# A transformer block pair on one core: silus and table loads in the planner's account, grouped silus, sums and masks on VectorE, another order of projections

## The chip, the core and the metric

The kernel runs on one core of a Trainium2 chip. The core has TensorE (PE, matrix products), VectorE (DVE), ScalarE (ACT), GpSimd (POOL) and SyncE (SP, which issues DMAs here). Each has a queue of its own and works through it in order; semaphores tie the queues together. The metric is the time of one launch on the device in microseconds (us), the median of several runs.

## The reference, cut to what matters

Two blocks over a sequence of 512 tokens, model width 1024, all in float32.

```python
def first_block(x, ...):
    h = h + 0.5 * rmsnorm(swiglu(rmsnorm(h)))          # FFN 1, width 2816
    u = rmsnorm(h)
    z, xbc, dt_raw, q, k, v, gates = split(u @ w_in)   # "mix 1"
    xbc = silu(causal_dwconv(xbc, 4 taps) + b)         # x (2048), B, C (4 groups of 128)
    y = ssd_chunked(x, softplus(dt_raw), A, B, C) + D * x      # 32 heads in 4 groups, chunks of 128
    y = rmsnorm over each group of (y * silu(z))
    y_ssd = y @ w_branch
    y_att = rmsnorm(softmax(q1 k1) v - lam * softmax(q2 k2) v) @ w_att   # 8 heads, ALiBi, causal
    merged = sigmoid(g0) * y_ssd + sigmoid(g1) * y_att
    h = h + rmsnorm(merged @ w_out)
    h = h + 0.5 * rmsnorm(swiglu(rmsnorm(h)))          # FFN 2
def second_block(x, ...):                              # "mix 2", then FFN 3
    q, k, v = silu(causal_dwconv(...)); q, k = l2norm(q), l2norm(k)
    o_gdn = rmsnorm(gated_delta_rule_chunked(q, k, v, g, beta)) * silu(z)   # 8 heads, chunks of 64
    o_dsa = sparse attention over the top 128 keys of an indexer
    h = h + (sigmoid(ga) * o_gdn + sigmoid(gb) * o_dsa) @ w_out
    h = h + (silu(conv(gate)) * conv(val)) @ w_down    # FFN 3
    return rmsnorm(h)
```

In the chunked delta rule a unit triangular matrix of 64 x 64 is inverted by levels: each level multiplies masked parts of a matrix with the inverse found so far.

## The kernel before

Activations lie transposed, features on the 128 partitions and the 512 tokens along the free dimension. Each float32 product is made of three float32r products (high times high, high times low, low times high; L1651 to L1653), so a **panel**, 1024 x 128 of a weight, is 8 x 3 = 24 matmuls of 128 x 128 x 512. A panel comes by DMA into one of 3 buffers `raw`, ScalarE rounds it (L1992) and VectorE subtracts to get the low part (L2289, tile `hl`, 3 buffers).

The work of a core is a list of steps, `plan`. Each engine's program walks that list once and issues its part of each step, so the plan's order is the order of every queue. What is emitted when is decided while the kernel is built. In the FFNs it is a plain loop. In mix 1 and mix 2 `schedule` (L705) runs a **main stream**, the projections, and **side streams**, the chains of small operations behind them (`ssd_side`, `att_side`; `scan_side`, `prep_side`, `index_side`). It asks the side streams first; a side stream goes on when `ready` (L383) says that the step's inputs are there by the account and that neither VectorE's nor ScalarE's account is more than `AHEAD` ahead of TensorE's. Else two k-blocks (6 matmuls) of the main stream are emitted. The account is `clock`, one time for each engine, which `spend` (L371) moves on by the costs that `costs` and `COSTS` give for a step's kind; a kind that has no entry costs nothing, and what it makes counts as ready at once.

The main stream's order is a string (L24, L25): in mix 1 `t` projects dt, `g0` to `g3` the x, B and C of a group (4 + 1 + 1 panels, each followed by a convolution of 4 taps and a silu), `z0` to `z3` the gates of a group (4 panels), `a` and `c` an attention head (3 panels; `c` waits for the head four before it), `b` the branch product of a gated group (16 half panels; it waits until the group is gated), `E` and `F` output gates, and `r8` waits until 8 pages are free. In mix 2 `p` is a pair of delta-rule heads (6 panels), `z` the two gates of a pair (4), `x` and `k` the indexer and the keys and values, `d` a sparse head's query, `h` waits until a pair is prepared. Pages are tiles of 128 x 512 in SBUF: 35 in mix 1, 38 in mix 2. The panels of dt, z0 and B of group 0 are made in the passage before mix 1 and lie in pages (`ahead`).

A group's chain in mix 1: four transposes with a scaling by dt (`ssd_x`, VectorE L2475), C times B (`ssd_cb`, TensorE L1723), states, then four rounds over pairs of heads (`ssd_from`, `ssd_front`, `ssd_mask`, `ssd_y`, TensorE L1759), then `gate_group` (L931): y times silu(z), squares on ScalarE, three additions on GpSimd (`sum4`, L2910), a product with a matrix of ones on TensorE (`rstd`, L1690), logarithm and exponential on ScalarE, and the gated tiles. Attention of a head: scores (L1786), softmax on VectorE and ScalarE, transposes of the probabilities (`pv_turn`, TensorE L1772, copied out by ScalarE, L2167), product with v (`pv_mul`, L1778). In mix 2 `gdn_seed` and `gdn_level` mask a tile for each level on GpSimd (L2924, L2931).

ScalarE must have a table set loaded that holds the function it evaluates; `activate` (L1970) issues a load (L1973) where the set in place doesn't hold it. Silu, exponential with logarithm, and exponential with tanh lie in different sets.

Before, a convolution's silu is issued in the middle of the next panel, and z's silu reads the bank that the product is in:

```python
            if q == STEP:
                flush()
...
            G["z"].append(evict("silu_ev", b))
```

Of the kernel before, what the change touches and what calls it, by code (L numbers as in the profile page):

```python
# [7 lines left out]
F = mybir.dt.float32  # L8
# [24 lines left out]
TABLES = {ACT.Ln: ("natural_log_exp_and_others",), ACT.Exp: ("natural_log_exp_and_others", "exp_and_others"),  # L33
          ACT.Silu: ("silu_and_others",), ACT.Tanh: ("silu_and_others", "exp_and_others"), ACT.Sigmoid: ("silu_and_others",)}
# [88 lines left out]
def costs(s):  # L123
# [8 lines left out]
    if k == "rstd":  # L132
        return [("PE", 0.9 * len(s["src"]), "pe_norm.sum"), ("ACT", 0.7, "act_norm.ln"), ("ACT", 0.63, "act_norm.r")]
    if k == "squares":
        return [("ACT", 0.62, "act_norm.sq", n) for n in range(len(s["src"]))]
    if k == "att_front":
        return [("PE", 0.33 * w), ("DVE", 0.45 + 0.58 * w), ("ACT", 0.5 + 0.22 * w, "act_att.P", 1)]
# [13 lines left out]
    if k == "sp_front":  # L151
        return [("PE", 0.14 * w), ("DVE", 0.45 + 0.27 * w), ("ACT", 0.4 + 0.11 * w, "act_spa.P")]
# [8 lines left out]
    "silu_ev": [("ACT", 0.63, "act_ev.out")], "tanh_ev": [("ACT", 0.63, "act_ev.out")],  # L161
# [3 lines left out]
    "sum4": [("POOL", 1.4, "pool_norm.sum4", 0), ("POOL", 1.4, "pool_norm.sum4", 1), ("POOL", 1.4, "pool_norm.sum4", 2)],  # L165
# [7 lines left out]
    "decay": [("DVE", 0.7), ("ACT", 0.63), ("DVE", 0.42), ("ACT", 0.63), ("DVE", 0.7), ("ACT", 0.63), ("DVE", 2.7), ("ACT", 0.2),  # L173
              ("DVE", 1.7, "dve_ssd.scan"), ("ACT", 0.62), ("DVE", 0.69, "dve_ssd.aclo")],
    "decay_turn": [("PE", 1.6, "pe_ssd.decay"), ("DVE", 0.9, "dve_ssd.alast"), ("ACT", 0.25), ("DVE", 0.3),
                   ("ACT", 0.3, "act_ssd.ddec")],
# [4 lines left out]
    "ssd_front": [("PE", 0.59), ("DVE", 0.69, "dve_ssd.seg"), ("DVE", 0.43), ("ACT", 0.65, "act_ssd.E")],  # L181
# [3 lines left out]
    "ssd_from": [("PE", 1.6, "pe_ssd.off"), ("ACT", 0.65, "act_ssd.EA"), ("DVE", 0.56, "dve_ssd.EA"), ("DVE", 0.56, "dve_ssd.off")],  # L185
    "ssd_y": [("PE", 1.03, "pe_ssd.y"), ("DVE", 0.69, "dve_ssd.y")],
    "turn_v": [("PE", 0.45, "pe_att.turn_v"), ("ACT", 0.6, "act_att.V")],
    "narrow": [("DVE", 0.9), ("ACT", 0.63), ("DVE", 1.1), ("ACT", 0.63), ("DVE", 0.42), ("ACT", 0.63), ("DVE", 0.7), ("ACT", 0.63),
               ("DVE", 5.0, "dve_gdn.nar")],
    "narrow_turn": [("PE", 4.1, "pe_gdn.iw"), ("ACT", 2.2, "act_gdn.cols", 1), ("ACT", 0.6, "act_gdn.iw")],  # L190
    "l2": [("DVE", 0.75, "dve_gdn.l2")],
    "gdn_decay": [("PE", 1.0), ("DVE", 0.69, "dve_gdn.seg"), ("DVE", 0.43), ("ACT", 0.65, "act_gdn.gm")],
# [3 lines left out]
    "gdn_seed": [("DVE", 1.4, "dve_gdn.U0"), ("POOL", 1.35, "pool_gdn.A", 0), ("POOL", 1.35, "pool_gdn.A", 1)],  # L196
    "gdn_seed_turn": [("PE", 1.15), ("ACT", 0.6, "act_gdn.T")],
    "gdn_level": [("PE", 1.07, "pe_gdn.Y"), ("ACT", 0.6, "act_gdn.Y"), ("POOL", 1.3, "pool_gdn.mask")],
# [6 lines left out]
    "gdn_norm": [("ACT", 1.25), ("DVE", 1.0, "dve_gdn.sum"), ("ACT", 0.45), ("DVE", 1.4, "dve_gdn.on")],  # L205
# [15 lines left out]
def build(nc, d, out):  # L221
# [137 lines left out]
    clock = dict.fromkeys(("PE", "ACT", "DVE", "POOL"), 0.0)  # L359
    at = {}  # L360
# [10 lines left out]
    def spend(s):  # L371
# [4 lines left out]
        if s.kind == "split" and s.j - NHL in ends:  # L376
            t = max(t, when(("pe_gemm.mm", *ends[s.j - NHL])))
        for engine, us, *name in costs(s):
            t = clock[engine] = max(clock[engine], t + 0.06) + us
            if name:  # L380
                at[(name[0], s.id, name[1] if len(name) > 1 else 0)] = t
# [18 lines left out]
    waiting = []  # L400
# [36 lines left out]
    def ugemm(src):  # L437
# [39 lines left out]
    def group_rstd(src, which):  # L477
# [5 lines left out]
        qs[1].release(("pool_norm.sum4", s2, 0))  # L483
        qs[3].release(("pool_norm.sum4", s2, 1))
        qs[2].release(("pool_norm.sum4", s2, 2))
        yield from ready(("pool_norm.sum4", s2, 2), banks=1)
        r = rstd([(qs[0][:, :], [("pool_norm.sum4", s2, 2)])], which)
# [157 lines left out]
    def conv(b, wname, taps, col, ncol, bias, silu, to=None, half=0):  # L645
        p = fp.take()
        flush()
# [3 lines left out]
    def conv_taps():  # L651
        if waiting and "s" not in waiting[0]:
            w = waiting[0]
# [7 lines left out]
    def flush():  # L661
        conv_taps()
        if waiting:
            w = waiting.pop()
            step("conv_silu", c=w["s"])
            t = ("act_conv.silu", w["s"])
            if w["to"] is None:
                w["p"].t = [t]
            else:
                w["p"].release(t)  # L670
                w["to"].t = w["to"].t + [t]
# [100 lines left out]
    s_con = step("ids")  # L772
    S1 = {}
# [27 lines left out]
    def project_group(g):  # L801
# [12 lines left out]
        yield  # L814
        flush()
        G["C"] = C
        G["xs"] = xs
# [105 lines left out]
    def project_z(g):  # L923
        G = grp[g]
        G["z"] = []
# [305 lines left out]
    def project_zg(h):  # L1231
        b = yield from ugemm(W2[24 + h])
# [1842 lines left out]
```

## Time and profile before

| | |
|---|---|
| median of 3 runs | 2760.79 us (2757.55 to 2762.05) |
| the profiled execution | 2757.5 us, span 2755.7 us |
| mean granted clock of TensorE | 0.973 |
| busy: TensorE, VectorE, ScalarE, GpSimd | 94%, 56%, 40%, 2% |
| FFN 1, mix 1, FFN 2, mix 2, FFN 3 (us, about) | 12 to 385, 385 to 1212, 1212 to 1670, 1670 to 2345, 2345 to 2755 |
| table loads of ScalarE | 95 |

A row of the windows gives the busy time of each engine in a stretch; the length less TensorE's busy time is its idle time. The granted clock is the share of full speed, 2.4 GHz, at which TensorE was clocked in the stretch. In a timeline the number in brackets is the idle time of the engine before the row's first instruction, with the instruction that ended it.

### The profile page before, as it was taken

How to read it: one execution, taken by the hardware profiler on the slowest of the kernel's cores; microseconds unless marked ns; L12 is line 12 of the kernel's file. 1: busy time of each engine (PE TensorE's matmuls, PEld its weight loads, DVE VectorE, ACT ScalarE, POOL GpSimd, SP SyncE). 2: the span in 40 equal slices, each digit the busy share in tenths (PEclk: the TensorE clock that was granted, in tenths of full speed). 3: DMA queues.
4: the chain of work that ended last, by engine and by line, in shares of the span. 5: the costliest groups of instructions: out<-in, count | busy, mean ns of one | idle time of the engine just before them, and what ended most of it. 6: DMA issues, size and time to landing. Idle time of an engine off the chain costs nothing.

```text
span 2755.7 us, 33784 instructions
## 1 busy us (share of the span) xinstructions
PE 2583.9 (94%) x13762; PEld 2037.0 (74%) x13762; DVE 1534.9 (56%) x2406; ACT 1111.1 (40%) x1684; POOL 44.9 (2%) x44
## 2 busy tenths in 40 slices
PE   7999998988899899899999999899999997999998
PEld 6888876666677677587888887677677675888886
DVE  5444257555666455535544327688765454677732
ACT  4223234545344445634322225543433355444421
POOL 0000000000000000000000000000000000000000
PEclk9999999999999999999999999999999999999999
DMA  4233322111121222122222332111111111323332
GB/s 138 97 100 96 98 91 71 54 46 61 54 65 58 69 70 66 56 85 92 92 96 95 96 97 85 62 47 62 46 56 39 55 54 39 99 93 100 96 94 78
DMA packets 59193, 209.93 MB, mean 76 GB/s; under 512 B 6560, under 2 KB 6560, under 8 KB 59040
## 3 DMA queue, kind: packets, MB, share of 16 engines
q1 hardware_dynamic: 57600, 204.38, 23.3%
q10 hardware_dynamic: 1440, 3.41, 0.4%
q8 instruction: 109, 1.79, 0.3%
q14 instruction: 44, 0.36, 0.0%
HBM read 205.66 MB, written 2.10 MB: 75 GB/s over the span
## 4 chain that ended last, share of the span: by engine, by line
PE 71%; DVE 15%; ACT 10%; issue 3%; POOL 1%; DMA 0%; DVEq 0%; SPq 0%; ACTq 0%
PE bank L1651 20%; PE bank L1653 19%; PE bank L1652 19%; DVE hl L2289 3%; ACT L1973 3%; ACT hl L1992 2%; ACT fB L1975 2%; DVE fB L2417 2%; ACT fA L1975 2%; PE bank L1853 1%; PE bank L1690 1%; PE bank L1778 1%; DVE fA L2417 1%; PE bank L1666 1%; PE bank L1668 1%
## 5 line engine op out<-in xcount | busy, mean ns | idle before, releaser
L1651 PE MATMUL bank<-uR,hl 128*128 128x512 f32 x2160 | 883.4, 409 | 25.9 <-DVE uR L2301 11.8
L1652 PE MATMUL bank<-uR,hl 128*128 128x512 f32 x2160 | 850.0, 394 | 0.0
L1653 PE MATMUL bank<-uR,hl 128*128 128x512 f32 x2160 | 850.0, 394 | 0.0
L2289 DVE TENSOR_TENSOR hl<-raw,hl 128x1024 fp32r<-128x1024 f32 (+1 forms) x391 | 472.1, 1208 | 621.4 <-ACT hl L1992 620.3
L1651 PEld LDWEIGHTS bank<-uR,hl 128*128 128x128 f32 x2160 | 411.2, 190 | 145.7 <-issue 41.7
L1992 ACT CAST hl<-raw 128x1024 fp32r<-128x1024 f32 (+1 forms) x391 | 401.5, 1029 | 207.7 <-PE bank L1653 195.5
L1653 PEld LDWEIGHTS bank<-uR,hl 128*128 128x128 f32 x2160 | 410.4, 190 | 88.7
L1652 PEld LDWEIGHTS bank<-uR,hl 128*128 128x128 f32 x2160 | 411.5, 191 | 86.7 <-issue 6.6
L1651 PE MATMUL bank<-act,hl 128*128 128x512 f32 x528 | 206.6, 391 | 0.0
L1653 PE MATMUL bank<-act,hl 128*128 128x512 f32 x528 | 205.5, 389 | 0.0
L1652 PE MATMUL bank<-act,hl 128*128 128x512 f32 x528 | 205.4, 389 | 0.0
L1973 ACT ACT_TABLE_LOAD x95 | 121.9, 1283 | 182.7 <-DVE fB L2417 39.2
L2294 DVE TENSOR_TENSOR fA<-bank,fA 128x512 f32<-128x512 f32 x132 | 90.9, 690 | 137.4 <-PE bank L1653 133.7
L1975 ACT ACTIVATE fA<-fA 128x512 f32<-128x512 f32 (+1 forms) x120 | 75.5, 631 | 213.9 <-DVE fA L2294 123.7
L2059 ACT CAST act<-fA 128x512 fp32r<-128x512 f32 x66 | 41.0, 621 | 284.1 <-DVE fA L2384 194.0
L1651 PE MATMUL bank<-mR,hl 128*128 128x512 f32 x320 | 129.2, 404 | 0.1
L1653 PE MATMUL bank<-mR,hl 128*128 128x512 f32 x320 | 125.3, 391 | 0.0
L1652 PE MATMUL bank<-mR,hl 128*128 128x512 f32 x320 | 125.1, 391 | 0.0
L1652 PEld LDWEIGHTS bank<-act,hl 128*128 128x128 f32 x528 | 99.1, 188 | 21.3 <-issue 0.7
L1651 PEld LDWEIGHTS bank<-act,hl 128*128 128x128 f32 x528 | 99.1, 188 | 21.2 <-issue 0.7
L1653 PEld LDWEIGHTS bank<-act,hl 128*128 128x128 f32 x528 | 99.1, 188 | 20.5
L1975 ACT ACTIVATE fB<-fB 128x512 f32<-128x512 f32 (+1 forms) x97 | 60.3, 629 | 107.5 <-DVE fB L2417 52.9
(454 smaller groups left out, 2689.4 us busy)
## 6 DMA issues: line engine op xcount, KB each, us to landing
raw<-in_win SPq DMA_DIRECT2D x147, 512.0 KB, 3.5
raw<-in_w SPq DMA_DIRECT2D x44, 512.0 KB, 3.5
raw<-in_w1g SPq DMA_DIRECT2D x22, 512.0 KB, 3.4
raw<-in_w1u SPq DMA_DIRECT2D x22, 512.0 KB, 3.4
raw<-in_w2g SPq DMA_DIRECT2D x22, 512.0 KB, 3.4
raw<-in_w2u SPq DMA_DIRECT2D x22, 512.0 KB, 3.5
raw<-in_w1d SPq DMA_DIRECT2D x16, 512.0 KB, 3.5
raw<-in_wssd SPq DMA_DIRECT2D x16, 512.0 KB, 3.4
```

Source lines behind the costliest of these rows:

```text
L1651: e.matmul(s.bank[:, :], h[:, 0, w], hi, start=s.first and q == 0, stop=False)
L1652: e.matmul(s.bank[:, :], h[:, 0, w], lo, start=False, stop=False)
L1653: i = e.matmul(s.bank[:, :], h[:, 1, w], hi, start=False, stop=s.last and q == n - 1)
L1666: e.matmul(b[:, :], h[:, 0, w], uR[:, 0, k, :], start=k == 0, stop=False)
L1668: e.matmul(b[:, :], h[:, 1, w], uR[:, 0, k, :], start=False, stop=False)
L1973: e.preload_act_table_set(sets[0])
L1975: return e.activation(o, i, func, **k)
L1992: e.copy(hl[j % NHL][:, 0, 0:s.width], raw[j % NRAW][:, 0:s.width]).then_inc(*sig("act_split.hi", s))
L2059: e.copy(s.a[:, 0, s.j, :], s.p[:, :]).then_inc(*sig("act_ffn.hi", s))
L2289: e.tensor_tensor(h[:, 1, 0:s.width], x[:, 0:s.width], h[:, 0, 0:s.width].bitcast(F), ALU.subtract).then_inc(*sig("dve_split.lo", s))
L2294: e.tensor_tensor(s.x[:, :], s.b[:, :], s.r[:, :], ALU.mult).then_inc(*sig("dve_norm.scaled", s))
L2417: e.scalar_tensor_tensor(out=s.p[:, i:L], in0=s.b[:, 0:L - i], scalar=pc(s.w, (s.taps - 1 - i) * s.ncol + s.col), in1=s.p[:, i:L], op0=ALU ...
```

## The change

Six things. The account (`spend`) also holds the silus, the norm steps and the passage's first products, and it charges 1.3 us for a table load when a step's function isn't in the set in place. A group's silus are collected and issued together, two after each quarter of a following panel (`due`); z is first copied out of its bank by ScalarE (or lies in a page already) and gets its silu there. A tanh takes the set of the exponential if a load is needed at all. The group norm's additions and the level masks go from GpSimd to VectorE. The order strings and `AHEAD` differ. In mix 2 `project_zg` waits for 6 free pages. The core of the diff:

```diff
-AHEAD = 3.0
+AHEAD = 6.0
-ORDER1 = "t g0 g1 z0 r8 z1 b0 g2 r8 z2 b1 g3 r8 a0 a1 b2 z3 r8 a2 a3 c4 b3 c5 c6 c7 E F"
-ORDER2 = "n p0 x p1 z0 h0 p2 z1 h1 p3 z2 k z3 d0 d1"
+ORDER1 = "t z0 g0 z1 g1 r12 g2 z2 b0 a0 g3 b1 a1 b2 z3 a2 a3 c4 c5 b3 c6 c7 E F"
+ORDER2 = "n p0 p1 x z0 h0 z1 p2 r10 z2 p3 d0 z3 r12 k r10 d1"
...
-          ACT.Silu: ("silu_and_others",), ACT.Tanh: ("silu_and_others", "exp_and_others"), ...}
+          "Silu": ("silu_and_others",), "Tanh": ("exp_and_others", "silu_and_others"), ...}
...
-    "silu_ev": [("ACT", 0.63, "act_ev.out")], "tanh_ev": [("ACT", 0.63, "act_ev.out")],
+    "silu_ev": [("ACT Silu", 0.63, "act_ev.out")], "tanh_ev": [("ACT Tanh", 0.63, "act_ev.out")],
+    "conv_silu": [("ACT Silu", 0.63, "act_conv.silu")], "silu_z": [("ACT Silu", 0.63, "act_ev.z")],
+    "scale": [("DVE", 0.62, "dve_norm.scaled")], "norm_x": [("DVE", 5.4, "dve_norm.x", 7)],
+    "norm_u": [("ACT", 0.6), ("DVE", 5.0, "dve_norm.lo", 7)], "lead": [("PE", 17.0, "pe_gemm.mm", 2)],
-    "sum4": [("POOL", 1.4, "pool_norm.sum4", 0), ...],
+    "sum4": [("DVE", 0.66, "dve_norm.sum4", n) for n in range(3)],
-    "gdn_level": [("PE", 1.07, "pe_gdn.Y"), ("ACT", 0.6, "act_gdn.Y"), ("POOL", 1.3, "pool_gdn.mask")],
+    "gdn_level": [("PE", 1.07, "pe_gdn.Y"), ("ACT", 0.6, "act_gdn.Y"), ("DVE", 0.5, "dve_gdn.mask")],
...
+        if s.kind == "conv_silu":
+            t = max(t, when(("dve_conv.tap", s.c, s.c.taps - 1)))
         for engine, us, *name in costs(s):
-            t = clock[engine] = max(clock[engine], t + 0.06) + us
+            engine, _, func = engine.partition(" ")
+            t = max(clock[engine], t + 0.06)
+            if func and clock["table"] not in TABLES[func]:
+                clock["table"] = TABLES[func][0]
+                t += 1.3
+            t = clock[engine] = t + us
...
-            if q == STEP:
+            if q == STEP and not batch[0]:
                 flush()
+            for x in range(min(2, len(due))):
+                due.pop(0)()
...
     def conv(b, wname, taps, col, ncol, bias, silu, to=None, half=0):
         p = fp.take()
-        flush()
+        conv_taps()
...
     def flush():
         conv_taps()
+        for w in waiting:
+            silu(w)
+        waiting.clear()
...
     def schedule(main, sides):
-        start = max(clock.values())
-        clock.update({x: start for x in clock})
+        for x in ("ACT", "DVE", "POOL"):
+            clock[x] = max(clock[x], clock["PE"])
...
     def project_group(g):
-        yield
-        yield
-        flush()
-        G["C"] = C
-        G["xs"] = xs
+        yield
+        conv_taps()
+        for w in waiting:
+            due.append(lambda w=w: silu(w))
+        waiting.clear()
+        due.append(lambda: G.update(C=C, xs=xs))
...
     def project_z(g):
         for i in range(4):
+            here = id(WIN[4 * g + i]) in ahead
             b = yield from ugemm(WIN[4 * g + i])
-            G["z"].append(evict("silu_ev", b))
+            z.append(b if here else evict("qkv_ev", b, scale=None))
             yield
+        def silu_z(x):
+            x.t = [("act_ev.z", step("silu_z", x=x, xt=list(x.t)))]
+        for x in z:
+            due.append(lambda x=x: silu_z(x))
+        due.append(lambda: G.update(z=z))
...
     def project_zg(h):
+        yield from room(6)
...
         def gdn_seed(s):                                  # VectorE's program
             e.tensor_tensor(v8(s.U), chunks8(cc(1, "id64")), v8(s.U), ALU.subtract)...
+            for n in range(2):
+                after(*s.A[n].after)
+                e.tensor_tensor(v8(s.A[n]), v8(s.AT), chunks8(con[1][:, ...]), ALU.mult)...
+        def gdn_level(s):
+            if s.lev < 4:
+                at = CCOLS["level"][0] + 64 * (s.lev + 2)
+                go.wait_ge(*on("pe_gdn.Y", s))
+                e.tensor_tensor(v8(s.A), v8(s.AT), chunks8(con[1][:, at:at + 64]), ALU.mult)...
```

`sum4` moves to VectorE's program word for word, and GpSimd's `sum4`, `gdn_seed` and `gdn_level` go. `batch[0]` is set before mix 1 and cleared before FFN 3, where a silu is issued in the next panel as before. In mix 2 the three silus of a delta-rule head are issued together at its end.

## Rows read from the trace of the kernel before

**Rows 1.** The page, busy time, share and instructions of each engine over the span.
```profile
PE 2583.9 (94%) x13762; PEld 2037.0 (74%) x13762; DVE 1534.9 (56%) x2406; ACT 1111.1 (40%) x1684; POOL 44.9 (2%) x44
```

**Rows 2.** Windows: length, busy us of PE, PEld, DVE, ACT, POOL; PEclk; DMA.
```profile
385.00:842.00 457.00, 405.45 (x1832) 304.33 (x1833) 291.82 (x429) 208.63 (x288) 13.58 (x13) 0.92 0.19 59
842.00:1212.00 370.00, 339.85 (x1555) 260.03 (x1552) 191.14 (x387) 183.69 (x353) 4.75 (x3) 0.96 0.21 67
1690.00:2140.00 450.00, 424.01 (x4045) 320.77 (x4045) 322.87 (x594) 189.32 (x285) 25.77 (x20) 0.99 0.17 55
2140.00:2345.00 205.00, 182.02 (x969) 139.90 (x969) 105.33 (x250) 96.14 (x198) 0.00 (x0) 0.97 0.16 49
2345.00:2700.00 355.00, 355.00 (x1565) 293.56 (x1565) 220.79 (x275) 139.19 (x180) 0.00 (x0) 1.00 0.31 97
```

**Rows 3.** Waits of TensorE: tile and line, releaser; total us, times, longest us.
```profile
PE bank L1778 <- ACT fA L2167: 17.6, 6, 6.5
PE bank L1778 <- ACT fB L2167: 16.4, 7, 5.1
PE bank L1723 <- DVE fB L2475: 15.5, 3, 6.0
PE bank L1690 <- POOL fA L2910: 12.6, 2, 7.8
...
PE bank L1690 <- POOL fB L2910: 12.0, 2, 6.3
```

**Rows 4.** Timeline of TensorE: start, us, operation, idle before it and releaser.
```profile
562.67 2.04 PE L1690 MATMUL bank<-fB,onesc 128*128 128x512 f32 x2 [5.73 <-POOL fB L2910]
...
573.60 2.05 PE L1723 MATMUL bank<-fA,fB 128*128 128x128 f32 x8 [4.97 <-DVE fB L2475]
```

**Rows 5.** Timeline of TensorE just after that second wait.
```profile
578.00 0.56 PE L1651 MATMUL bank<-mR,hl 128*128 128x512 f32 x1
578.40 0.39 PE L1652 MATMUL bank<-mR,hl 128*128 128x512 f32 x1
578.62 0.39 PE L1653 MATMUL bank<-mR,hl 128*128 128x512 f32 x1
```

**Rows 6.** Timeline of ScalarE, then of GpSimd, before the wait at 562.67.
```profile
559.03 0.61 ACT L1975 ACTIVATE fB<-fB 128x512 f32<-128x512 f32 x1
...
558.69 1.27 POOL L2910 TENSOR_TENSOR fB<-fB,fA 128x512 f32<-128x512 f32 x1 [172.33 <-ACT fA L1975]
559.92 2.61 POOL L2910 TENSOR_TENSOR fB<-fB 128x512 f32<-128x512 f32 x2
```

**Rows 7.** Timeline of GpSimd and of VectorE at the fourth sum.
```profile
921.39 2.25 POOL L2910 TENSOR_TENSOR fA<-fA,fB 128x512 f32<-128x512 f32 x1
...
921.29 1.23 DVE L2289 TENSOR_TENSOR hl<-raw,hl 128x1024 fp32r<-128x1024 f32 x1 [4.26 <-ACT hl L1992]
```

**Rows 8.** Lines, 385:1212 ScalarE, 1690:2345 ScalarE, 385:1212 VectorE, 1690:2345 GpSimd.
```profile
L1973 ACT ACT_TABLE_LOAD x53 | 68.0, 1283 | 101.9 <-DVE small L2587 29.3 <-DVE fB L2417 21.8 <-PE bank L1690 19.5
...
L2147 ACT COPY fB<-bank 128x512 f32<-128x512 f32 x10 | 5.8, 581 | 7.6 <-PE bank L1653 7.6
...
L1973 ACT ACT_TABLE_LOAD x38 | 48.8, 1283 | 72.8 <-DVE fA L2417 18.4 <-DVE fB L2417 17.4 <-DVE small L2853 12.8
...
L2511 DVE TENSOR_TENSOR fB<-fB 128x512 f32<-128x512 f32 x16 | 10.4, 684 | 0.0
...
L2931 POOL TENSOR_TENSOR gx<-gx,con 128x512 f32<-128x512 f32 x12 | 15.6, 1301 | 166.6 <-PE bank L1853 166.6
```

**Rows 9.** Timeline of ScalarE in the last part of mix 2.
```profile
2288.11 1.28 ACT L1973 ACT_TABLE_LOAD   x1 [2.50 <-DVE small L2853]
2289.41 0.72 ACT L1975 ACTIVATE fB<-fB,small 128x512 f32<-128x512 f32 x1
```

**Rows 10.** Timeline of TensorE, the products of two rounds of one group following.
```profile
825.34 0.66 PE L1759 MATMUL bank<-fB 128*64 128x128 f32 x8
...
835.10 0.66 PE L1759 MATMUL bank<-fA,fB 128*64 128x128 f32 x8
```

More of the change, by code:

```diff
@@ L359, in build @@
     clock = dict.fromkeys(("PE", "ACT", "DVE", "POOL"), 0.0)
+    clock["table"] = ""
     at = {}
@@ L482, in group_rstd @@
         s2 = step("sum4", qs=qs, s=s)
[L483 to L487, printed above, removed]
+        qs[1].release(("dve_norm.sum4", s2, 0))
+        qs[3].release(("dve_norm.sum4", s2, 1))
+        qs[2].release(("dve_norm.sum4", s2, 2))
+        yield from ready(("dve_norm.sum4", s2, 2), banks=1)
+        r = rstd([(qs[0][:, :], [("dve_norm.sum4", s2, 2)])], which)
         qs[0].release(("pe_norm.sum", r.s))
@@ L651, in conv_taps @@
     def conv_taps():
-        if waiting and "s" not in waiting[0]:
-            w = waiting[0]
+        if waiting and "s" not in waiting[-1]:
+            w = waiting[-1]
             w["s"] = s = step("conv", **w)
@@ L662, in flush, with silu @@
         conv_taps()
[L663 to L671, printed above, removed]
+        for w in waiting:
+            silu(w)
+        waiting.clear()
+    def silu(w):
+        step("conv_silu", c=w["s"])
+        t = ("act_conv.silu", w["s"])
+        if w["to"] is None:
+            w["p"].t = [t]
+        else:
+            w["p"].release(t)
+            w["to"].t = w["to"].t + [t]
     def value(gen):
@@ L772, in build @@
     s_con = step("ids")
+    batch[0] = True
     S1 = {}
@@ L1970, in activate @@
         def activate(o, i, func, **k):
-            sets = TABLES.get(func)
+            sets = TABLES.get(func.name)
             if sets and table[0] not in sets:
@@ L2134, in silu_ev, with silu_z @@
             activate(s.p[:, :], s.b[:, :], ACT.Silu).then_inc(*sig("act_ev.out", s))
+        def silu_z(s):
+            after(*s.xt)
+            activate(s.x[:, :], s.x[:, :], ACT.Silu).then_inc(*sig("act_ev.z", s))
         def tanh_ev(s):
@@ L2529, in gate, with sum4 @@
                 e.tensor_tensor(s.z[i][:, :], s.z[i][:, :], s.Y[i][:, :], ALU.mult).then_inc(*sig("dve_ssd.gate", s, i))
+        def sum4(s):
+            q = s.qs
+            for n, (i, j) in enumerate(((0, 1), (2, 3), (0, 2))):
+                go.wait_ge(*on("act_norm.sq", s.s, 3 if n else 1))
+                if n == 2:
+                    go.wait_ge(*on("dve_norm.sum4", s, 1))
+                e.tensor_tensor(q[i][:, :], q[i][:, :], q[j][:, :], ALU.add).then_inc(*sig("dve_norm.sum4", s, n))
         def gate_out(s):
@@ L2916, in ssd_sel @@
                           con[0][0:32, 8 * s.g:8 * s.g + 8][:, :, None].broadcast_to([32, 8, 64])).then_inc(*sig("pool_ssd.sel", s))
-        def gdn_seed(s):
-            lv = CCOLS["level"][0]
-            go.wait_ge(*on(*con_in[1]))
-            after(*s.AT.t)
-            for n in range(2):
-                after(*s.A[n].after)
-                e.tensor_tensor(v8(s.A[n]), v8(s.AT), chunks8(con[1][:, lv + 64 * (n + 1):lv + 64 * (n + 2)]),
-                                ALU.mult).then_inc(*sig("pool_gdn.A", s, n))
-        def gdn_level(s):
-            if s.lev < 4:
-                at = CCOLS["level"][0] + 64 * (s.lev + 2)
-                go.wait_ge(*on("pe_gdn.Y", s))
-                e.tensor_tensor(v8(s.A), v8(s.AT), chunks8(con[1][:, at:at + 64]), ALU.mult).then_inc(*sig("pool_gdn.mask", s))
-        do = {"init": init, "sum4": sum4, "ssd_sel": ssd_sel,
-              "gdn_seed": gdn_seed, "gdn_level": gdn_level}
+        do = {"init": init, "ssd_sel": ssd_sel}
         for s in plan:
```

61 lines of the change are left out of this document (29 added, 32 removed).

## The prediction

> **What bounds the kernel now.** I read the page first: TensorE is busy 94% of the span, VectorE 56%, ScalarE 40%, GpSimd 2% [rows 1]. So the time is TensorE's work, which the change leaves as it is (no matmul is added or dropped), plus its idle time, 2755.7 - 2583.9 = 171.8 us, plus what it loses at a lowered clock. The windows by stage say where: in 2345 to 2700, the third FFN, it is busy 355.00 of 355.00 us at granted clock 1.00; 1565 matmuls in 355 us make 0.227 us each, and a panel of 24 makes 5.4 us. In mix 1 it idles 51.5 + 30.2 = 81.7 us at a granted clock of 0.92 and 0.96, in mix 2 26.0 + 23.0 = 49.0 us at 0.99 and 0.97 [rows 2]. The other 41 us lie at the start, the end and the passages between stages, which the change leaves alone. So it works on 130.7 us of idle time and on the clock behind it.
>
> The list of waits tells what TensorE waits for: the copies of attention tiles that ScalarE makes (L1778, 17.6 + 16.4 = 34.0 us in 13 waits), the sum of squares that GpSimd makes (L1690, 12.6 + 12.0 = 24.6 us in 4), and VectorE's scaled x of a group (L1723, 15.5 us in 3) [rows 3]. The remaining 130.7 - 74.1 = 56.6 us are single and small waits. The timeline shows two long ones in a row, 5.73 us ending at 562.67 and 4.97 us ending at 573.60 [rows 4]. Behind the second the matmuls start 0.40 us apart at 578.00 and 0.22 us apart from 578.40 on [rows 5]: these are the two levels of the clock, 1.2 and 2.4 GHz. From 573.60 to 578.2 it thus ran at half rate, which is a loss of 4.6 / 2 = 2.3 us for a long wait beside the wait.
>
> TensorE's program is one queue in the order of the plan. Where the plan thinks a result ready too early, TensorE stands at that instruction with panels behind it that could have run. Where the plan holds the main stream, there is nothing behind it. Both kinds are in the rows: at 562.67 the stream had done z1 and was held until group 0 was gated, since "b0" follows "z1".
>
> **The change part by part.** All terms are against the profiled execution's own 2757.5 us; the median of the runs is 2760.8, which is 3.3 more.
>
> *Sums of squares on VectorE.* The last square ends at 559.03 + 0.61 = 559.64, GpSimd's last addition at 559.92 + 2.61 = 562.53 [rows 6]: 2.9 us. An addition of two tiles of this shape takes VectorE 0.684 us [rows 8], and two of them follow the last square: 1.4 us. That saves 1.5 us in each of 4 groups, and 1.0 more in the fourth, whose last addition took GpSimd 2.25 us while VectorE's subtraction of 1.23 us ran [rows 7]: 7 us. The other 17.6 us go only if panels stand in their place. The new order has "g2 z2" ahead of "b0", 10 panels or 54 us that need nothing of the gate; and the account now knows of silus, table loads and the additions' engine, so that it puts the norm later. I take 13 of 17.6, and three of four losses of 2.3 us: 13 + 7 + 7 = 27 us. Bounds: 7, and 24.6 + 9.2 = 34.
>
> *Silus and table loads in the account, waits at L1723.* Before, a conv's silu cost the account nothing, and its end counted as ready at once, so the x of a group was called early. I take half of the waits, 8 us, and half of three clock losses, 3: 11 us, with bounds 0 and 15.5 + 6.9 = 22. I take the half because the other part of these waits, the four multiplications by D and VectorE's queue, is priced as it was.
>
> *Fewer table loads.* ScalarE makes 53 of them in mix 1 and 38 in mix 2, 1.283 us each [rows 8]. Silus of a group made together need one pair of loads where each silu between exponentials needed one, and a tanh now takes the set in which the exponential lies too. I estimate that 40 of 91 go: 51 us of ScalarE. What that is worth is read from the end of mix 2: there VectorE's row is ready, ScalarE loads for 1.28 us, then makes the exponential [rows 9], and TensorE has no panels left to put between. Of the 34.0 us at L1778 I take half, and two clock losses: 17 + 5 = 22 us. Bounds: four such loads in bare stretches, 5 us; and all of it, 34 + 4 x 2.3 = 43.
> The row shows 2288.11 + 1.28 = 2289.39 as the load's end and 2289.41 as the start of what follows [rows 9]. The Trainium skill (ScalarE: Activation LUTs, "What ACT_TABLE_LOAD costs") adds about 1.38 us of draining to each switch of sets, 2.66 us in all. The trace doesn't agree. By the page 40 loads would be 106 us instead of 51, and the same share of it another 22 us off the time.
>
> *Early start of attention, attention heads spread earlier in the order, AHEAD 6.* With "a0", "b1", "a1" spread between the groups and fewer holds ahead of them, core 3 can end earlier and attention has more panels beside it. Of the remaining 56.6 us I take 5 as gain, between -15 (work of the side streams called 6 us ahead of VectorE's queue comes too early more often) and +25.
>
> *What is added.* VectorE gets 12 additions and 8 + 12 masks of 0.684 us, 21.9 us; the masks took GpSimd 1.30 us each [rows 8]. ScalarE gets 12 copies of z out of a bank at 0.581 us, 7.0 us [rows 8]. Their cover is that VectorE is busy 64% and 72% in the stretches concerned (292 of 457, 323 of 450 us), ScalarE 46% and 42% [rows 2]. The masks stand in VectorE's queue just ahead of the subtractions that close a level, while TensorE does the level's products, so they cost when VectorE is behind already. I take a quarter of VectorE's and little of ScalarE's: -6 us; bounds 0 and -29. The deferred silus come two at a time between panels' quarters of 1.4 us, which ScalarE can hold.
>
> *What is held.* "r12" after "g1" holds the main stream until 12 pages are free. Of 35, group 0's z, x and C, z1, g1 and the core's own tiles take about 30, so it opens when the first core ends. Before, the stream stood at about the same place for other reasons (15 panels were done when core 0 ended). In mix 2, 14 panels stood behind "p3" (z2, k, z3, d0, d1), now 10 do, with "r12" and "r10" between. I take -5; bounds 0 and -42 (worked out below).
>
> Sum: 27 + 11 + 22 + 5 - 6 - 5 = 54 us. 2757.5 - 54 = 2703.5, and 3.3 more for the median: 2707.
>
> **Rivals.**
> *Only what became shorter counts (2741 us).* The plan is another guess, wrong in other places, and new waits replace old ones. Then 7 us of the additions remain, 5 to 20 us of table loads, -6 of what was added; with some luck in the order 20 us: 2761 - 20 = 2741. For it: a large part of the waits (multiplications by D, VectorE's backlog of conv taps) is priced as before. Against it: the waits at L1690 have one cause, and it is taken away.
>
> *The main stream is held (2775 us).* Two rounds of a core follow each other in 835.10 - 825.34 = 9.8 us [rows 10]; 24 matmuls of panels, 5.4 us, lie between. Bare of panels, a round idles up to 5.4 us. Two bare rounds behind "r12" are 10.9 us and two clock losses 4.6; in mix 2 four panels fewer beside the last scan leave 21.8 and 4.6: 42 us. At three fifths of this price, 25 us, against the 11 us that are saved in any case (7 + 10 - 6), it is 2761 + 14 = 2775. It decides from 17 us of such idle time on, if the account's part brings nothing. For it: no page is gained and the order now leans on free pages four times late or in long stretches. Against: the order before held as often ("r8" four times, "h0", "h1").
>
> *Nearly all goes (2658 us).* If the account is now right, two thirds of 130.7 us and of 14 clock losses of 2.3 (32 us) go, 109 us, less 6: 2761 - 103 = 2658. For it: between 385 and 842 VectorE and ScalarE are far from full, so the waits are of order, not of work. Against: the end of each mix has chains with few panels left.
>
> *Table loads cost twice (2685 us).* ScalarE would be later behind each of them than the row's 1.28 us; 22 us more than the forecast. The row speaks against it.
>
> **How the numbers follow.** Forecast 0.48, with a range of its own from 2685 to 2727; only what became shorter 0.22 (2727 to 2756); nearly all 0.14; held 0.11; table loads twice 0.02; no change at all 0.03. The likeliest gives 2707. The range goes from 2662 to 2768: below it lies about half of "nearly all", above it most of "held". A change is told from none at 0.2%, 5.5 us, to be counted once here: faster 0.48 + 0.14 + 0.02 + most of 0.22 = 0.82; the same 0.07; slower 0.11.
>
> **What would show it.** Right: no wait of TensorE at L1690 for the sums over 2 us; under 60 table loads; idle time of mix 1 under 50 us and its granted clock over 0.95; the FFN stages as before. Wrong: in the timeline of TensorE more than 12 us idle between the last panel of g1 and the first of g2, or during the last scan of mix 2; waits for L2289 (hl) over 3 us, which would be VectorE full of sums and masks; idle time of the mixes that is still over 110 us.

## The result

The changed kernel takes 2622.66 us (median of 4 runs, 2619.71 to 2624.43) against 2759.17 us (4 runs, 2755.31 to 2762.05) of the kernel before in the same comparison: a ratio of 0.9505 with a 95% interval from 0.9489 to 0.9522. The gain is 136.5 us. The forecast was 54, and the time lies 39 us below the range. The same line of code stands 28 lines lower in TensorE's part of the new file, and 28 to 50 lower in the parts behind it.

The page's first part, after. It answers to [rows 1].

```profile
PE 2534.8 (97%) x13762; PEld 2013.2 (77%) x13762; DVE 1549.4 (59%) x2438; ACT 1060.3 (41%) x1654; POOL 3.6 (0%) x12
```

TensorE does the same 13762 matmuls in 49.1 us less, and its idle time went from 171.8 to 2617.9 - 2534.8 = 83.1 us, 88.7 less. The two make the 137.8 us by which the profiled execution is shorter. The forecast had 15 us for the first, the clock.

The windows of the two mixes, of the kernel after, then of the kernel before, each from the mix's first product to the first of the stage behind it (columns as in [rows 2]). Mix 1 is longer here than in the table ahead, which ends it at 1212 us: its output product runs to 1299.6.

```profile
383.10:1194.00 810.90, 790.55 (x3742) 610.09 (x3743) 528.73 (x877) 394.04 (x673) 2.79 (x4) 0.99 0.23 74
1564.50:2207.20 642.70, 614.19 (x5084) 473.32 (x5085) 454.42 (x888) 280.81 (x487) 0.00 (x0) 0.99 0.17 55
```

```profile
384.60:1299.60 915.00, 828.79 (x3742) 631.76 (x3742) 524.49 (x865) 428.64 (x691) 18.33 (x16) 0.94 0.21 66
1670.50:2345.00 674.50, 624.33 (x5084) 475.37 (x5085) 445.23 (x869) 297.15 (x499) 25.77 (x20) 0.98 0.16 53
```

Mix 1 became 104.1 us shorter: idle time 86.2 to 20.4, busy time 828.8 to 790.6 with the same 3742 matmuls, granted clock 0.94 to 0.99. Mix 2 became 31.8 shorter: idle time 50.2 to 28.5, busy time 624.3 to 614.2 with the same 5084. Together that is 135.9 of the 137.8 us; FFN 1 is 1.5 us shorter, the other two FFN stages agree within 0.5 us. VectorE's work in the mixes went up by 4.2 + 9.2 us, ScalarE's down by 34.6 + 16.3.

The waits of TensorE after, longest first. They answer to [rows 3].

```profile
PE bank L1679 <- DVE uR L2333: 11.9, 1, 11.9
PE bank L1694 <- ACT uR L2062: 11.2, 3, 3.7
PE bank L1679 <- DVE hl L2321: 8.4, 4, 4.9
PE bank L1913 <- DVE gx L2760: 6.7, 1, 6.7
...
PE bank L1806 <- ACT fB L2199: 3.5, 5, 1.3
...
PE bank L1718 <- DVE fB L2569: 1.5, 1, 1.5
```

The first three are as before (the passages, 11.9 and 11.2 us, and 8.4 for cast weights, the longest again 4.9). L1718 (before L1690) waits 1.5 us for sums, once, where it was 24.6. L1806 (before L1778) waits 3.5 here and 1.0 more elsewhere, where it was 34.0. L1751 (before L1723, 15.5 us) is no longer in the list.

ScalarE's table loads in mix 1 and in mix 2, and VectorE's additions, to set against [rows 8] and [rows 6].

```profile
L2001 ACT ACT_TABLE_LOAD x23 | 29.5, 1283 | 21.6 <-DVE fB L2539 6.3 <-DVE small L2627 5.4 <-DVE small L2496 5.2
```

```profile
L2001 ACT ACT_TABLE_LOAD x25 | 32.1, 1283 | 38.5 <-PE bank L1681 16.4 <-DVE small L2805 9.0 <-PE bank L1718 4.5
```

```profile
L2569 DVE TENSOR_TENSOR fA<-fA,fB 128x512 f32<-128x512 f32 x4 | 2.7, 689 | 0.4 <-ACT fB L2003 0.3
```

53 and 38 loads became 23 and 25, 43 fewer, and the addition takes 0.689 us. Both sizes are as forecast (40 loads, 0.684 us). What they are worth is another matter.

The loads that went are of two kinds. Some stood between a silu and an exponential. The others stood between a tanh and an exponential of attention, since before a tanh took silu's set. ScalarE in mix 2 of before (start, length), ahead of a wait of TensorE of 4.09 us that ends at 2314.64:

```profile
2309.09 0.40 ACT L1975 ACTIVATE fB<-fB,small 128x128 f32<-128x128 f32 x1 [2.47 <-DVE small L2853]
2309.39 0.19 ACT L1975 ACTIVATION_READ_ACCUMULATOR fB<-fB,small 128x1 f32 x1
2309.60 1.28 ACT L1973 ACT_TABLE_LOAD   x1
2310.89 0.69 ACT L1975 ACTIVATE fB<-bank,small 128x512 f32<-128x512 f32 x1
2311.60 1.28 ACT L1973 ACT_TABLE_LOAD   x1
2312.89 0.51 ACT L1975 ACTIVATE fB<-fB,small 128x256 f32<-128x256 f32 x1
```

The load at 2309.60 is for the tanh of an output gate (read out of a bank), the one at 2311.60 brings the exponential's set back, and the copy that TensorE waits for comes behind both.

What is to be seen besides, and explains the largest part of the gain, is what ScalarE waited for. In the rows of before, 21.8 us of the idle time ahead of the table loads of mix 1 and 18.4 + 17.4 of mix 2 were ended by VectorE's L2417 [rows 8]. That is the line of the conv taps. The whole span of before, ScalarE, by groups (idle time before them, by releaser, is the last column):

```profile
L1973 ACT ACT_TABLE_LOAD x95 | 121.9, 1283 | 182.7 <-DVE fB L2417 39.2 <-DVE fA L2417 31.2 <-DVE small L2587 29.3
L1975 ACT ACTIVATE fA<-fA 128x512 f32<-128x512 f32 (+1 forms) x120 | 75.5, 631 | 213.9 <-DVE fA L2294 123.7 <-DVE fA L2417 78.2 <-DVE fA L2507 10.9
L1975 ACT ACTIVATE fB<-fB 128x512 f32<-128x512 f32 (+1 forms) x97 | 60.3, 629 | 107.5 <-DVE fB L2417 52.9 <-DVE fB L2507 45.5 <-DVE fB L2664 3.5
```

Added up from the trace between 385 and 2345 us, 48 silus of the mixes waited 182.7 us for L2417, 17 of them at the table load that goes ahead of them (the expectations below say 184.7). In the changed kernel 9 do, for 22.0 us, all in mix 2. Another 22 such waits, 46 us, lie in FFN 3, before as after. How such a wait gets to TensorE is seen at 469 us of before: ScalarE, then VectorE, then TensorE (start, length, and in brackets the idle time before and what ended it).

```profile
465.42 0.63 ACT L1975 ACTIVATE fA<-fA 128x512 f32<-128x512 f32 x1 [2.88 <-DVE fA L2417]
465.96 0.76 ACT L1975 ACTIVATE fB<-bank,par 128x512 f32<-128x512 f32 x1
469.10 0.63 ACT L1975 ACTIVATE fB<-fB 128x512 f32<-128x512 f32 x1 [2.38 <-DVE fB L2417]
469.64 1.03 ACT L1992 CAST hl<-raw 128x1024 fp32r<-128x1024 f32 x1
```

```profile
466.75 2.32 DVE L2417 SCALAR_TENSOR_TENSOR fB<-bank,par,fB 128x511 f32<-128x511 f32 x3 [1.36 <-ACT fB L1975]
470.76 1.23 DVE L2289 TENSOR_TENSOR hl<-raw,hl 128x1024 fp32r<-128x1024 f32 x1 [1.70 <-ACT hl L1992]
471.91 2.48 DVE L2475 TENSOR_TENSOR fB<-bank,small 128x512 f32<-128x512 f32 x4
```

```profile
472.74 1.62 PE L1723 MATMUL bank<-fB,fA 128*128 128x128 f32 x6 [5.98 <-DVE fB L2475]
```

ScalarE starts the conv of C at 465.96 and has its silu next in its program. The silu needs the three taps, which VectorE makes from 466.75 to 469.07, so ScalarE stands for 2.38 us and the cast of the next weights (L1992) stands behind it; that cast ends at 470.67, and VectorE, after 1.70 us of waiting for it, subtracts (L2289) and only then comes to L2475, for which TensorE has waited 5.98 us. Two engines hand each other the wait. Of the 5.98 us, 1.70 are VectorE's wait for the cast; the taps and the subtraction ahead of L2475 would be in its queue in any case.

### The profile page after: what moved, and what is told of

Its sections match the earlier page's. It is cut to its first block and busy times, and to the rows that moved or that the text cites. A ratio compares the mean times of both kernels' runs of the same rounds, so it can differ in the third digit from the quotient of the medians.

```text
span 2617.9 us, 33764 instructions
## 1 busy us (share of the span) xinstructions
PE 2534.8 (97%) x13762; PEld 2013.2 (77%) x13762; DVE 1549.4 (59%) x2438; ACT 1060.3 (41%) x1654; POOL 3.6 (0%) x12
## 3 DMA queue, kind: packets, MB, share of 16 engines
q1 hardware_dynamic: 57600, 204.38, 24.6%
## 5 line engine op out<-in xcount | busy, mean ns | idle before, releaser
L1679 PE MATMUL bank<-uR,hl 128*128 128x512 f32 x2160 | 875.5, 405 | 25.4 <-DVE uR L2333 11.9
```

What stands on the lines that cost most here:

```text
L1679: e.matmul(s.bank[:, :], h[:, 0, w], hi, start=s.first and q == 0, stop=False)
```

## The experiments

Two theories at the start. A: the account (silus and table loads in it) made the plan right. B: some part of what ScalarE does became cheaper or shorter. After the first four runs B split in two: T, the table loads that grouping saves, and Q, the queue just shown. Ratios are to the kernel before in the same comparison, whose median ran from 2757.7 to 2769.9 us over the comparisons (single runs from 2755.3 to 2771.0); what one edit is worth is the difference of two kernels' own medians. The runs of the other kernels scatter by 1 to 6 us, so a difference to the kernel before is less sure than one between two others.

**e1, VectorE's part alone, on the kernel before.**
```diff
-    "sum4": [("POOL", 1.4, "pool_norm.sum4", 0), ...
+    "sum4": [("DVE", 0.66, "dve_norm.sum4", n) for n in range(3)],
   (sum4, the masks and A of gdn_seed and gdn_level moved to vector_program)
```


> The kernel before with one part of the change: the group norm's additions and the level masks on VectorE (and priced there in the account). Theory A (the account): the gain of 136 us comes from steps being called when they are ready; moving these operations shortens four chains by 1.5 us each and adds 22 us of work to VectorE, so the time stays within 12 us of before (2747 to 2765), and TensorE's waits at the sum of squares keep at least half of their 24.6 us. Theory B (shorter work): the four waits of 24.6 us and their clock losses of 9 us go, 2725 to 2735.

2742.41 us (2741.03 to 2747.02), ratio 0.9929 [0.9908, 0.9951]: 20 us, by the interval 14 to 25, and between the two expectations. TensorE's waits at the norm (L1690) from mix 1 on fell from 37.3 us to 19.2, those for the sums alone from 24.6 to 6.2; those at L1778 stayed (35.0). In the profiled executions mix 1 became 16.2 us shorter (915.0 to 898.8) and mix 2, where the masks are, 5.5 longer (674.5 to 680.0).

**e2, the changed kernel with both old orders.**
```diff
-ORDER1 = "t z0 g0 z1 g1 r12 g2 z2 b0 a0 g3 ...
+ORDER1 = "t g0 g1 z0 r8 z1 b0 g2 r8 z2 b1 g3 ...
   (and ORDER2 as before)
```


> The changed kernel with the two order strings of before. Theory A (the account): the waits of TensorE stay few (under 25 us in the two mixes) and the time is 2635 to 2665, since the order only decides how much the main stream is held. Theory C (the order): the waits were a matter of which panel stands beside which chain; with the old order at least half of the gain is lost, 2690 or more.

2662.71 us (2659.32 to 2663.77), ratio 0.9636 [0.9613, 0.9658]: the orders are worth 40.1 us, as theory A had it. Idle time is 108.8 us, table loads 46.

**e3, e2 with an account that sees neither silus nor tables.**
```diff
-    "conv_silu": [("ACT Silu", 0.63, ...)], "silu_z": [...],
-                t += 1.3
```


> As the run with the old order strings, and the account again without silus (conv_silu, silu_z cost nothing) and without the charge for table loads; the silus are still made in groups and the sums are on VectorE. Theory A (the account): steps are called too early again, TensorE's waits in the mixes rise over 60 us and the time is at least 40 us above the run with the old order alone, 2690 to 2730. Theory B (shorter work: fewer table loads, sums on VectorE): within 15 us of the run with the old order alone.

2663.09 us (2660.48 to 2665.24), ratio 0.9639 [0.9616, 0.9662]: no difference to e2, though it makes 58 table loads to e2's 46. Theory A falls for the old order, as far as silus and table loads in the account go; the norm steps and the starts in it stayed.

**e4, e2 with the silus one by one as before, z's made from its bank.**
```diff
             if q == STEP and not batch[0]:
                 flush()          # batch[0] stays False in both mixes
```


> As the run with the old order strings, and the silus again one by one in the panel that follows, z's silu out of the bank; the account knows of all silus and table loads. Theory A (the account): waits of TensorE stay few (under 40 us in the mixes), but the true cost of 90 table loads holds the streams more; 2690 to 2730, better than before. Theory B (shorter work): the number of table loads decides, it is near 95 again, and the time is within 20 us of before, 2740 or more.

2735.28 us (2730.48 to 2736.56), ratio 0.9897 [0.9874, 0.9921]: grouping is worth 72.6 us, more than the whole forecast. The time lies between the ranges of both theories. Mix 1 is 30.0 us longer than in e2 and mix 2 42.6; there it is also 32.4 us longer than in the kernel before, so single silus cost more under this plan than they did before. Yet there are only 62 table loads to e2's 46. Of the 95 of the kernel before, 33 are gone without any group: this kernel has tanh in the exponential's set.

**e5, e4 with the silus as Identity** (the silu is left out of the result; place, length and waits stay. FFN 3's are Identity too; that stage takes 410.7 us in both).
```diff
-                activate(c.p[:, :], c.p[:, :], ACT.Silu)
+                activate(c.p[:, :], c.p[:, :], ACT.Identity)
```


> The kernel of e4 (old order, silus one by one, 2735.3 us, 62 table loads), plan unchanged, in which the silus of the two mixes are computed as Identity: this leaves the silu out of the result and with it the switches of ScalarE's tables that a silu forces, while every silu's instruction keeps its place, its length and its wait for VectorE's conv taps. Theory T (the grouping of silus pays by its table loads): table loads fall by 25 or more and most of the 72.6 us between e4 and e2 comes, 2663 to 2690 us. Theory Q (it pays by the queue: ScalarE works in order, a silu that stands right behind its own conv waits there for VectorE's taps, and the casts, evictions and exponentials behind it wait with it): at most 1.3 us for each load that goes and little of that, 2705 to 2733 us, and ScalarE's idle time in front of the silus' line stays within a tenth of e4's.

2707.09 us (2704.45 to 2708.34), ratio 0.9793 [0.9773, 0.9812], with 27 loads: 28.2 us for 35 loads, 0.8 us each. Q said so; ScalarE's waits of silus for the taps in the mixes are 155.7 us in 48, as in e4 (155.3). The loads of tanh were gone in e4 already, so this prices silu's loads only.

**e6, e4 with each silu alone, one panel later.**
```diff
             if q == STEP:
-                flush()
+                for w in [w for w in waiting if w.get("n", j) < j]:
+                    silu(w)
+                    waiting.remove(w)
   (w["n"] is the panel at whose start the taps were issued)
```


> The kernel of e4 with each conv's silu still issued alone, but one panel later than before (in the second step of the panel after the one whose second step issued it), so that the taps are done when ScalarE comes to it; nothing is grouped, z's silus stay as in e4. Theory Q: 2660 to 2685 us, most of the 72.6 us between e4 and e2 without a group, and ScalarE's idle time in front of the silus falls below a third of e4's. Theory T: table loads stay at 55 or more and the time within 12 us of e4's 2735.

2668.09 us (2667.06 to 2668.57), ratio 0.9652 [0.9630, 0.9674]: 67.2 of the 72.6 us, with 70 table loads, more than e4 has. This is Q and not T. The edit holds in FFN 3 too, which stays at 410.7 us. The groups of ScalarE in e4 and then in e6:

```profile
L1992 ACT ACT_TABLE_LOAD x62 | 79.5, 1283 | 106.8 <-DVE fB L2440 26.1 <-DVE fA L2440 24.1 <-PE bank L1672 18.4
L1994 ACT ACTIVATE fA<-fA 128x512 f32<-128x512 f32 (+1 forms) x117 | 73.7, 631 | 230.4 <-DVE fA L2317 123.7 <-DVE fA L2440 88.2 <-DVE fA L2530 9.3
L1994 ACT ACTIVATE fB<-fB 128x512 f32<-128x512 f32 (+1 forms) x93 | 58.2, 630 | 119.9 <-DVE fB L2530 49.2 <-DVE fB L2440 44.8 <-DVE fB L2695 10.7
```

```profile
L1996 ACT ACT_TABLE_LOAD x70 | 89.8, 1283 | 90.0 <-PE bank L1713 17.0 <-PE bank L1676 14.4 <-DVE small L2800 11.3
L1998 ACT ACTIVATE fA<-fA 128x512 f32<-128x512 f32 (+1 forms) x119 | 74.6, 628 | 149.0 <-DVE fA L2321 124.1 <-DVE fA L2534 14.9 <-DVE fA L2444 4.4
L1998 ACT ACTIVATE fB<-fB 128x512 f32<-128x512 f32 (+1 forms) x98 | 61.3, 630 | 65.2 <-DVE fB L2534 42.1 <-DVE fB L2790 11.6 <-DVE fB L2444 8.4
```

L2440 and L2444 are the conv taps. They end 26.1 + 24.1 + 88.2 + 44.8 = 183 us of e4's idle time in these groups, and 4.4 + 8.4 us in e6, with 7.8 more at table loads that the row has no room for. In e4 46 us of them lie in FFN 3, in waits of 2.1 us; they are gone in e6, and the stage is no shorter. In the mixes alone, all tiles counted, such waits are 155.3 us in e4 and 41.1 us, 22 waits, in e6.

**e7, the changed kernel with mix 2's old order.**
```diff
-ORDER2 = "n p0 p1 x z0 h0 z1 p2 r10 z2 p3 d0 z3 r12 k r10 d1"
+ORDER2 = "n p0 x p1 z0 h0 p2 z1 h1 p3 z2 k z3 d0 d1"
```


> The changed kernel with the old order of mix 2's projections only. The two old orders together cost 40.1 us (e2 against the changed kernel). If mix 1's order brings them: 2622 to 2632 us. If mix 2's does: 2650 to 2663. If both do, half each: 2638 to 2646, which I expect, since the gap between the changed kernel and e2 lies in both mixes.

2639.88 us (2639.67 to 2640.16), ratio 0.9551 [0.9533, 0.9569]: mix 1's order brings 22.8 us, mix 2's 17.2.

**e8, e2 with additions and masks back on GpSimd** (the reverse of e1's edit).

> The kernel of e2 (old order, 2662.7 us) with the additions of the norm's squares and the seed masks back on GpSimd. The same move alone on the kernel before was worth 19.6 us (e1). If its worth is its own (waits of TensorE for the sums, which nothing else covers): 2678 to 2690 us, with waits of TensorE for GpSimd of over 15 us together. If it only counted because the mixes were late anyway: 2660 to 2670 us.

2682.71 us (2681.97 to 2683.30), ratio 0.9705 [0.9687, 0.9724]: 20.0 us, as in e1. Here both mixes are longer than in e2, by 13.9 and 6.6 us: beside the new account and AHEAD 6 the masks no longer cost on VectorE. The first wait of its list is TensorE's for GpSimd's additions:

```profile
PE bank L1718 <- POOL fB L2942: 15.1, 4, 7.0
```

**e9, the kernel before with e6's edit alone.** The diff is e6's, with `waiting[-1]` for `waiting[0]` where taps are issued.

> The kernel before with one edit: each conv's silu is issued alone, one panel later; account, order, GpSimd's work and AHEAD are as before. Theory Q (the wait behind the silu is what the kernel before paid most for, whatever plans it): e6 showed 67.2 us for this edit, so 2690 to 2710 us, the table loads stay above 80, and ScalarE's waits for the conv taps in the mixes fall from 184.7 us below 45. If the edit pays only together with the changed account: 2740 us or more.

2704.53 us (2702.41 to 2705.04), ratio 0.9790 [0.9766, 0.9814]: 56.1 us, by the interval 51 to 65, from one edit that saves six table loads and no other work. Mix 1 is 39.6 us shorter, mix 2 10.6, and FFN 3, whose silus are late too, as long as before. ScalarE after it, to set against the three rows of before above:

```profile
L1980 ACT ACT_TABLE_LOAD x89 | 114.2, 1283 | 123.0 <-DVE small L2594 29.5 <-PE bank L1697 19.6 <-DVE fB L2514 17.9
L1982 ACT ACTIVATE fA<-fA 128x512 f32<-128x512 f32 (+1 forms) x120 | 75.2, 628 | 146.9 <-DVE fA L2301 123.7 <-DVE fA L2514 14.9 <-DVE fA L2671 4.7
L1982 ACT ACTIVATE fB<-fB 128x512 f32<-128x512 f32 (+1 forms) x97 | 60.3, 629 | 67.0 <-DVE fB L2514 45.5 <-DVE fB L2424 12.4 <-DVE fB L2671 3.5
```

The waits of silus for the taps in the mixes are 47.2 us in 21 instead of 182.7 in 48, a little more than the 45 expected. 25.2 us of what is left are the eight silus of v (tile gx): a delta-rule head ends with a `flush`, so they still stand right behind their own conv. TensorE waits 7.1 us instead of 18.3 at the lines of L1723's step and 26.4 instead of 37.3 at the norm's. The attention copies did not move, 17.7 + 17.6 us:

```profile
PE bank L1785 <- ACT fB L2174: 17.7, 6, 7.3
PE bank L1785 <- ACT fA L2174: 17.6, 6, 6.5
```

**e10, e9 with e1's edit too.**

> e9 with the additions of squares and the seed masks on VectorE as well. If the two gains are independent, e9 less the 19.6 us of e1: 2670 to 2690 us. If the one covers the other: within 8 us of e9.

2695.29 us (2694.05 to 2696.20), ratio 0.9759 [0.9731, 0.9787]: 9.2 us more, between the two expectations. By stages it is much as in e1: against e9 mix 1 is 18.5 us shorter and mix 2 6.9 longer. Whether the later silus cover a part of e1's 20 us is not shown, as that figure hangs on the kernel before and its scatter.

**e11, e2 with the silus as Identity** (again without the silu in the result).

> The kernel of e2 (grouped silus, old order, 2662.7 us, 46 table loads) with the mixes' silus computed as Identity, which leaves the silu out of the result and its table switches with it; the plan is unchanged. e5 gave 28.2 us for 35 loads fewer where silus stood one by one, 0.8 us each. If each load costs that much anywhere: 2640 to 2650 us with some 22 loads. If loads cost little once ScalarE waits for no taps: 2655 to 2663 us, which I expect, since ScalarE is busy for 40% of the span only.

2662.70 us (2661.06 to 2663.22), ratio 0.9639 [0.9616, 0.9662], with 21 loads instead of 46: 0.0 us for 25 loads. Where no silu stands waiting in ScalarE's queue, the loads that silus bring are hidden.

**e12, e2 with AHEAD 3.0 instead of 6.0.**

> The kernel of e2 (AHEAD 6, 2662.7 us) with AHEAD 3 as in the kernel before. If AHEAD is a part of the gain (less of the side work starts too late): 2672 to 2690 us. If not, within 5 us of e2, 2658 to 2668.

2681.60 us (2680.87 to 2684.28), ratio 0.9710 [0.9687, 0.9734]: AHEAD is worth 18.9 us under the new account.

**e13, e10 with AHEAD 6.0**, the account still the old one.

> e10 (the kernel before with silus one panel later and the additions on VectorE, 2695.3 us, its account of engine times as before) with AHEAD 6. e12 showed 18.9 us for AHEAD under the new account. If AHEAD's worth needs no account: 2671 to 2682 us, and TensorE's waits at the products of weights and values (35.5 us in e10) fall below 12. Then the account and the grouping together are worth 8 to 19 us at most. If those waits go by the account: 2688 us or more.

2684.44 us (2680.77 to 2685.91), ratio 0.9729 [0.9714, 0.9743]: 10.9 us, less than I expected and more than the other case. The attention copies wait 20.4 us, before 35.6 in e10:

```profile
PE bank L1785 <- ACT fB L2174: 15.0, 10, 5.9
...
PE bank L1785 <- ACT fA L2174: 5.4, 4, 2.1
```

So AHEAD alone takes away 15 us of these waits; 13.0 us at the transposes just ahead of them (4.9 in e10) take part of their place.

**e14, e13 with the new order of mix 1.**

> e13 with the new order of mix 1's projections. Under the new account and the grouping this order was worth 22.8 us (e2 to e7). If its worth is its own: 18 to 28 us below e13. If it needs the group of silus or the account: within 8 us of e13.

2679.28 us (2676.61 to 2679.66), ratio 0.9709 [0.9693, 0.9725]: 5.2 us, not 23. The order needs the other parts.

**e15, e7 with an account that sees neither silus nor tables** (e3's edit).

> The kernel of e7 (changed kernel with mix 2's old order, 2639.9 us) whose account again holds neither the silus nor the tables, as e3 did it for e2 (663.1 against 2662.7: nothing; read 2663.1). If the new order of mix 1 pays by the grouping of silus alone: 2636 to 2646 us. If it pays because the account sees silus and tables: 2652 us or more, back towards e3.

2651.29 us (2648.64 to 2651.97), ratio 0.9569 [0.9553, 0.9585]: 11.4 us above e7 and 11.8 below e3, between the two cases. Silus and tables in the account are worth nothing beside the old order and 11 us beside the new one.

## Why the prediction was wrong

From the kernel before to the changed one, by medians (us off the time, 137.95 in all, since before's median beside e9 was 2760.61):

| step | runs | us |
|---|---|---|
| silus one panel later | before, e9 | 56.1 |
| sums and masks on VectorE | e9, e10 | 9.2 |
| AHEAD 6 | e10, e13 | 10.9 |
| the whole new account, tanh in the exponential's set, 6 free pages for `project_zg` | e13, e6 | 16.4 |
| group of silus in place of single late ones, z's silu apart | e6, e2 | 5.4 |
| order of mix 1 | e2, e7 | 22.8 |
| order of mix 2 | e7, after | 17.2 |

The parts lean on one another, so another path gives them other sizes (VectorE's part 20 us taken first; silus and tables in the account 0.4 us taken last before the orders, between e3 and e2, and 11 us after mix 1's order).

**The step that failed** is the pair "Silus and table loads in the account" and "Fewer table loads". It counted for the grouping only the loads that it saves (16 by e4 and e2, of the 43), and named the later silus as added work to be covered ("two at a time between panels' quarters"). The account was given 11 us; silus and tables in it bring 0.4 (e3, e2). The grouping's main effect stood in no term: a silu that is issued behind its own conv holds all of ScalarE until VectorE has made the taps. e9 measures it alone at 56.1 us, e4 against e2 at 72.6, e6 shows that lateness and not the group makes 67.2 of it. The rows ahead of the prediction carried the sign: 57.6 us of idle time ahead of table loads, ended by L2417 [rows 8]. The prediction used those rows for the count and length of the loads and did not ask what L2417 is.

*Table loads*: count and length were right (43 fewer for 40, 1.283 us), but the term did not tell two kinds apart. The loads of silus are worth 0.0 us for 25 in e11, and 0.8 us each in e5, where single silus make a queue that TensorE waits on. The loads between tanh and exponential are another matter, and no run changes them alone. The forecast gave the loads half of the 34.0 us at L1778. In the trace of before, loads fill 9.2 us of these waits, in 7 of the 13: six times next to a tanh, as in the rows at 2309 us, and once, at 898 us, next to a silu of z. In e1, e9 and e10 those loads are there and the waits are 35 us; AHEAD 6 took 15 of them in e13; from e13 to e6, with tanh in the new set and the new account, loads go from 89 to 70, the waits from 20.4 to 6.7 us, and the time by 16.4. In no kernel with the new set does one of these waits hold a load, nor with AHEAD 3 (e12, 10.3 us). How much of the 16.4 us is tanh's set and how much the account stays open, so this half of the term is neither shown nor refuted. Of the rival on loads that cost twice nothing is seen. The Trainium skill (ScalarE: Activation LUTs, "What ACT_TABLE_LOAD costs") gives 2.66 us for a switch; the rows at 2309 us show two switches with 0.02 us or less on either side of each load, so the trace doesn't show the page's draining.

*Waits at L1723*: forecast 11 us by the account, half of them left. All went. e9 takes 11.2 of 18.3 us at this step without touching the account, through the chain at 469 us. Left at this step are 7.1 us in e9, 9.5 in e10, 6.0 in e13, 4.4 in e3, 3.4 in e2, and nothing in e7, with the new order.

*Sums of squares on VectorE*: forecast 27 - 6 = 21 us with what is added; e1 gave 20, e8 20.0. The total was right and the masks did cost mix 2 some 6 us beside the old account (5.5 in e1, 6.9 in e10). The split was not: the forecast gave 7 us to the move itself and left the rest to panels of the new order, but with the old order e1 already took 18.4 of the 24.6 us of waits for the sums.

*The order*: forecast +5 and -5 us, measured 22.8 + 17.2. I had sought the stretch in which "r12" holds the stream; there is none of over 12 us. e14 and e15 tell why it could not be sized from the trace of before: beside single late silus and the old account mix 1's order brings 5.2 us; with groups, tanh's set and the account less silus and tables 11.8 (e3, e15); with the whole account 22.8. Which of its moves (z ahead of g, attention's heads spread, fewer holds) does it was not tried.

*The clock*: forecast 15 us for three single losses in the first term and a few in the others, measured 49.1 us of TensorE's busy time. I had priced a loss only behind a long wait. Over the large steps the busy time falls with the idle time: before to after 49.1 for 88.7, e4 to e6 30.0 for 37.7, e2 to after 17.4 for 25.7, before to e9 17.2 for 35.3. So 0.5 to 0.8 us came back for each us of idle time, small waits included. It is no fixed rate: before to e1 it is 1.2 for 9.6, and e6 is busy 2.5 us less than e2 with 7.5 more idle. The 49.1 for 88.7 of the whole change, applied to the 39 us of waiting time in the forecast, would have made it some 60 us, still short: the count of waits that go was the larger error.

*The rival "nearly all goes"* named the result but for its size: it took two thirds of the idle time of the mixes (87 us; measured 65.9 + 21.7 = 87.6) and of 32 us of clock, 21 us. Its condition, "if the account is now right", is not what brought the most: e9 has 56.1 us without it, and silus and tables in it bring 0.4 us beside the old order and 11.4 beside the new. That its idle time came out right is luck; its clock was 28 us short.

Of the signs of a right forecast all were seen (sums 1.5 us, 52 loads, mix 1 idle 20.4 us at 0.99, FFN stages unchanged). Of those of a wrong one, a wait for hl of over 3 us is there, 4.9 us, but it stood there before too. They could not tell 54 us from 137, since each had a bound on one side only.

Open: the 16.4 us between e13 and e6 in their parts, tanh's set above all, and which moves of the two orders make their 40 us.

## What to carry to other kernels

In a table of groups, read the releaser of the idle time before a cheap instruction as a question: what stands behind it in its engine's program? An operation of ScalarE that waits for VectorE's work on the same tile, issued right behind its own first half, blocks casts, evictions and exponentials that are ready; issue it a panel later, alone or in a group. It pays only where TensorE hangs on that queue: in FFN 3 the same waits, 46 us on ScalarE, went in e6 and e9 with nothing gained. Then see what the rest is worth, for the parts lean on one another: silu's table loads went from 0.8 us each to none with the queue, and mix 1's order from 5 to 23 us with the groups and the account. And split a count of table loads by the functions that cause them before pricing it.

## What the runs showed of the hardware

Twenty-five table loads of 1.283 us can go with no effect on the time (e11), and thirty-five cost 28 us (e5), in kernels that differ in where silus stand. The engine's instructions next to a load can stand 0.02 us or less from it (before, 2309 us). TensorE's busy time for the same 13762 matmuls ran from 2583.9 us (171.8 idle, mean granted clock 0.973) to 2534.8 us (83.1 idle, 0.992): over the whole change each us of idle time went with another 0.55 us of busy time.
